# Both layers' experts by seven products of quarters, first products ahead of down

## The chip, the cores and the metric

The kernel runs on one core of one Trainium2 chip, in fp32 throughout. The metric is the device time of one execution in microseconds (us); shown is the median of several. Engines are called as in the profile: PE is TensorE, PEld its weight loads, DVE VectorE, ACT ScalarE, POOL GpSimd, SP SyncE, which here only issues transfers.

## The reference

A trunk of two layers works on 1024 tokens of width 1024 (and 256 context rows in layer 0). Each layer has a mixer (layer 0: differential and neighbourhood attention; layer 1: windowed attention and a state space scan) and then a feed-forward part by 16 experts of which each chooses its rows. That part is all that the change touches in earnest:

```python
def expert_choice_ffn(h, w_router, w_gate, w_up, w_down):
    b, n, _ = h.shape
    cap = CAPACITY_FACTOR * n // N_EXPERTS
    aff = jax.nn.softmax(jnp.einsum('bnd,de->bne', h, w_router).astype(jnp.float32), axis=-1)
    gate, idx = lax.top_k(jnp.swapaxes(aff, 1, 2), cap)
    bidx = jnp.arange(b)[:, None, None]
    xg = h[bidx, idx]
    hid = jax.nn.silu(jnp.einsum('becd,edf->becf', xg, w_gate)) * jnp.einsum('becd,edf->becf', xg, w_up)
    out = jnp.einsum('becf,efd->becd', hid, w_down) * gate[..., None].astype(h.dtype)
    return jnp.zeros_like(h).at[bidx, idx].add(out)
```

Each expert takes 128 of the 1024 tokens; in layer 0 it takes 32 of the 256 context rows too. Its three weights are 1024x1024, 4 MB each, so 12 MB are read per expert, 16 times in each layer.

## The kernel before

The program is a chain of stages, one after the other; each stage has one instruction list per engine, ordered by semaphores, and a stage's end waits for all engines. Tiles that the next stage needs early are in "Ahead" objects: they are loaded by the stage before. The experts stage of layer 0 runs from about 1010 to 1947 us, that of layer 1 from about 2676 to the end.

**Layer 0: `experts` (L2357).** An expert's rows are gathered by POOL's indirect DMA (`gather`, L2494 ff.), turned by PE against the identity (`turn_rows`), scaled and shifted from PSUM into `xT` by ACT (four blocks) and DVE (four blocks, and the context's). `xT` holds 128 token columns and 32 context columns, 160 together. Then for each of eight groups of 128 hidden features PE does eight matmuls for gate and eight for up (`hidden_rows`, L2756) with the weight as the stationary operand and the 160 columns moving. ACT takes silu of the gate half, DVE multiplies it with the up half (`hidden`, L2653): the hidden rows come out turned already, as down needs them. Down (`down_rows`, L2722) multiplies them with two halves of 512 columns, and between the halves stands the context's down (`down_ctx`, L2731), in which four stationary tiles of 32 columns are worked on side by side. ACT and DVE scale the results by the row's weight into `y` and `yc`, and POOL adds them to `moe` in HBM by a scatter with addition: first `yc`, 1 KB rows, then `y`, 4 KB rows. In POOL's loop the next expert's gather stands ahead of the scatter, and behind a wait for the last scatter.

SP loads weights by halves of columns: gate's and up's first half as soon as four feature groups are done, their second half after eight, down's two halves once the down product is over. Around the loop the stage also finishes the modulation vectors: `opening` (16 steps at its beginning, with stores by SP: `store_third`) and `closing` (8 steps at its end, whose weights SP loads into the places of gate and up). Between the first experts' loads SP runs `following.load` (L2313), which fetches what the next stage (`front`) needs, many of these transfers in 4-byte pieces, and `following.load_columns`, 4 MB of the front's weights into `following.w`.

**Layer 1: `last_experts` (L2782).** Gate and up are multiplied by seven products instead of eight: rows and weights are cut into quarters (64 rows by 512, 512 by 512), and sums of quarters are multiplied (a Strassen scheme in Winograd's form). `PRODUCTS` (L2775) is the order of the products; product 1, 2 and 3 take a quarter of the weight as it is, 5, 6, 7 and 4 take sums that DVE makes (`weight_sum`, L3017 to L3026, each over 128x2048 elements); the row sums are `row_sums`. A product (`multiply`, L3159) is 8 matmuls with 64 stationary columns and 256 moving, two side by side. Bank Z takes 5 and 3, X takes 1, 6 and 7, W takes 2, V takes 4; ACT copies a bank out in the middle of its sum (`keep`, L2953), and DVE adds that copy to a finished bank (`quarter`, L3034). `QUARTERS` says which bank and which copy make which quarter. The hidden rows come out as rows and have to be turned (`turn_hidden`, L3123) and copied by ACT into `hT` (L2976) before down (L3167), which writes into W and V once more; ACT and DVE then copy these as `y` (L2986, L3086). So the next expert's product 2 must wait for `ya` (W is copied) and product 4 for `yv` (V is copied). PE's order in the loop is: gate's seven products, up's seven, turn half the hidden rows, turn the next expert's rows, turn the other half, down with its k steps outside.

SP loads layer 1's weights by halves of rows: gate's first half after product 7, its second after product 4, and so for up; down's after the two halves of its k steps. After the last expert's gate products it loads eight blocks of `res` (`load_rows`) and then the finished sums from `moe` (`load_sum`, L2884), of which ACT takes squares (`square`, L2958) between its bank copies; at the end DVE adds them to `res` (`gated`, `summed`, L3068).

## Time and profile before

| what | us |
|---|---|
| median of 3 runs | 3416.34 (3415.37 to 3417.86) |
| the profiled execution | 3414.7 |
| its span, first to last instruction | 3413.0 |
| PE busy | 3160.0, 93% of the span |
| DVE busy | 1559.8, 46% |
| ACT busy | 1009.8, 30% |
| gate and up matmuls of layer 0 (L2756) | 301.3 and 299.4 |
| layer 0's down matmuls (L2722) | 228.3 |
| layer 1's down matmuls (L3167) | 130.8 and 129.6 |

A record of a matmul in fp32 stands twice in the counts, since each is issued as two. In the timeline, instructions of one kind are merged: `xN` is how many, the first number is the start of the first and the second the time to the end of the last, which is modelled and reaches a little into the next group; so lengths are taken from start to start. In brackets stands the idle time of the engine before it, and who ended that.

### The profile page before, as it was taken

How to read it: one execution, taken by the hardware profiler on the slowest of the kernel's cores; microseconds unless marked ns; L12 is line 12 of the kernel's file. 1: busy time of each engine (PE TensorE's matmuls, PEld its weight loads, DVE VectorE, ACT ScalarE, POOL GpSimd, SP SyncE). 2: the span in 40 equal slices, each digit the busy share in tenths (PEclk: the TensorE clock that was granted, in tenths of full speed). 3: DMA queues.
4: the chain of work that ended last, by engine and by line, in shares of the span. 5: the costliest groups of instructions: out<-in, count | busy, mean ns of one | idle time of the engine just before them, and what ended most of it. 6: DMA issues, size and time to landing. Idle time of an engine off the chain costs nothing. (4 is left out here: it accounts for less than half of the span.)

```text
span 3413.0 us, 52595 instructions
## 1 busy us (share of the span) xinstructions
PE 3160.0 (93%) x19496; PEld 2216.1 (65%) x19496; DVE 1559.8 (46%) x3170; ACT 1009.8 (30%) x2323; POOL 525.1 (15%) x639
## 2 busy tenths in 40 slices
PE   6999989999987999999999799899899299999996
PEld 4888856667435788787887565666664155555553
DVE  3212178778654010101101254566785666666565
ACT  4111156755330111101111152235554222222222
POOL 0010235110100101011110120254101101111112
PEclk9999999999987999999999899999999599999998
DMA  6336353053639977787777630100414589999996
GB/s 231 130 108 114 92 188 113 20 132 95 241 132 339 352 267 250 244 275 245 265 255 262 232 121 1 56 22 28 112 33 173 197 293 334 326 335 339 338 335 257
DMA packets 340390, 672.38 MB, mean 197 GB/s; under 512 B 84041, under 2 KB 133065, under 8 KB 334017
## 3 DMA queue, kind: packets, MB, share of 16 engines
q1 hardware_dynamic: 308384, 568.00, 47.9%
q0 software_dynamic: 13616, 47.32, 5.5%
q10 hardware_dynamic: 18240, 55.16, 4.3%
q8 instruction: 83, 1.36, 0.2%
q14 instruction: 67, 0.54, 0.1%
HBM read 585.65 MB, written 90.97 MB: 198 GB/s over the span
## 5 line engine op out<-in xcount | busy, mean ns | idle before, releaser
L2756 PE MATMUL experts_gu_ps<-experts_xT,experts_wg 128*128 128x160 f32 x2048 | 301.3, 300 | 2.6 <-DVE experts_xT L2630 2.6
L2756 PE MATMUL experts_gu_ps<-experts_xT,experts_wu 128*128 128x160 f32 x2048 | 299.4, 299 | 0.0
L2756 PEld LDWEIGHTS experts_gu_ps<-experts_xT,experts_wg 128*128 128x128 f32 x2048 | 287.9, 191 | 9.9 <-issue 9.9
L2756 PEld LDWEIGHTS experts_gu_ps<-experts_xT,experts_wu 128*128 128x128 f32 x2048 | 285.6, 190 | 0.0
L2653 DVE TENSOR_TENSOR experts_hid<-experts_sil,experts_gu_ps 128x160 f32<-128x160 f32 x128 | 41.1, 321 | 516.1 <-ACT experts_sil L2584 516.1
L2722 PE MATMUL experts_y_ps<-down_ahead_wd,experts_hid 128*128 128x512 f32 x512 | 228.3, 599 | 0.0
L2584 ACT ACTIVATE experts_sil<-experts_gu_ps 128x160 f32<-128x160 f32 x128 | 38.9, 304 | 604.9 <-PE experts_gu_ps L2756 604.9
L2722 PEld LDWEIGHTS experts_y_ps<-down_ahead_wd,experts_hid 128*128 128x128 f32 x512 | 94.6, 190 | 114.4 <-issue 113.7
L3458 PE MATMUL front_pb_ps<-kept_hT,front_ahead_w 128*128 128x512 f32 (+1 forms) x384 | 138.7, 521 | 0.7 <-DVE kept_dt L3509 0.7
L3167 PE MATMUL experts_w_ps<-experts_wd,experts_hT 128*128 128x512 f32 x256 | 130.8, 597 | 8.5 <-issue 7.8
L3167 PE MATMUL experts_v_ps<-experts_wd,experts_hT 128*128 128x512 f32 x256 | 129.6, 592 | 0.0
L2671 DVE TENSOR_SCALAR experts_y<-experts_y_ps,experts_wt 128x512 f32<-128x512 f32 x16 | 12.0, 751 | 249.0 <-PE experts_y_ps L2722 249.0
L554 PE MATMUL proj_x_ps<-first_w,first_shared 128*128 128x256 f32 x480 | 115.0, 383 | 3.1 <-DMA first_w<-in_l_w_in 3.1
L3912 PE MATMUL scan_f_ps<-scan_w,kept_hT 128*128 128x512 f32 x256 | 116.4, 597 | 0.0
L3458 PEld LDWEIGHTS front_pb_ps<-kept_hT,front_ahead_w 128*128 128x128 f32 x384 | 72.4, 190 | 62.7 <-issue 59.4
L2524 POOL DMA_INDIRECT moe<-experts_yc,experts_ixsc x16 | 25.8, 1610 | 522.5 <-ACT experts_yc L2601 522.5
L2953 ACT ACTIVATE experts_kept<-experts_x_ps 128x256 f32<-128x256 f32 x96 | 36.8, 384 | 231.7 <-PE experts_x_ps L3159 230.4
L554 PEld LDWEIGHTS proj_x_ps<-first_w,first_shared 128*128 128x128 f32 x480 | 91.7, 192 | 15.9 <-DMA first_w<-in_l_w_in 3.4
L635 DVE TENSOR_TENSOR proj_ob<-proj_z_ps,proj_kept 128x256 f32<-128x256 f32 x30 | 12.7, 424 | 190.3 <-PE proj_z_ps L554 189.5
L867 ACT ACTIVATE attn_a_e<-attn_a_e,attn_a_nmx 128x1280 f32<-128x1280 f32 (+1 forms) x80 | 96.6, 1209 | 8.0 <-DVE attn_a_e L929 8.0
L3167 PEld LDWEIGHTS experts_w_ps<-experts_wd,experts_hT 128*128 128x128 f32 x256 | 47.3, 190 | 65.5 <-issue 64.5
L3167 PEld LDWEIGHTS experts_v_ps<-experts_wd,experts_hT 128*128 128x128 f32 x256 | 48.6, 190 | 61.2 <-issue 61.2
(561 smaller groups left out, 6308.7 us busy)
## 6 DMA issues: line engine op xcount, KB each, us to landing
experts_wg<-in_l_w_gate SPq DMA_DIRECT2D x64, 2048.0 KB, 8.5
experts_wu<-in_l_w_up SPq DMA_DIRECT2D x64, 2048.0 KB, 12.7
down_ahead_wd<-in_l_w_down SPq DMA_DIRECT2D x32, 2048.0 KB, 10.6
experts_wd<-in_l_w_down SPq DMA_DIRECT2D x32, 2048.0 KB, 7.7
down_ahead_wd<-in_l_w_mod SPq DMA_DIRECT2D x16, 1024.0 KB, 9.2
proj<-proj_ob ACTq DMA_DIRECT2D x60, 256.0 KB, 2.3
first_w<-in_l_w_in SPq DMA_DIRECT2D x6, 2048.0 KB, 10.1
attn_a_mod_w<-in_l_w_mod ACTq DMA_DIRECT2D x12, 1024.0 KB, 6.5
```

The costliest lines, as they stand in the source:

```text
L554: mm = nc.tensor.matmul(to[:, left], by[k], at[k], start=(k == 0 and n in (0, 1, 5)), stop=(k == HALF - 1 and n in (3, 5, 6)), skip_group_ ...
L635: nc.vector.tensor_tensor(ob[:, slot, 0, right], Z[:, left], kept[:, 2], ALU.add).then_inc(dve_out, 1)
L867: nc.scalar.activation(e[:, s, m, 0:w], e[:, s, m, 0:w], ACT.Exp, bias=nmx[:, s, m:m + 1], scale=-1.0, accum_out=sums[:, s, m:m + 1]).then ...
L2524: pool.indirect_dma_start(moe.rearrange("t (j c) -> (t j) c", j=4), bass.IndirectOffsetOnAxis(ap=ixsc[:, 0:1], axis=0), yc[:], None, compu ...
L2584: nc.scalar.activation(sil[:, f % 2, :], GU[f % 2][:, 0, 0:N], ACT.Silu).then_inc(sil_done, 1)
L2653: nc.vector.tensor_tensor(hid[:, f, :], sil[:, f % 2, :], GU[f % 2][:, 1, 0:N], ALU.mult).then_inc(hid_done, 1)
L2722: mm = nc.tensor.matmul(Y[h][:], hid[:, k, 0:CAPX], wd[:, h, k, :], start=(k == 0), stop=(k == KD - 1))
L2756: mm = nc.tensor.matmul(GU[f % 2][:, part, 0:N], w[:, h, k, c * P:(c + 1) * P], xT[:, k, :], start=(k == 0), stop=(k == KD - 1))
L2953: nc.scalar.activation(kept[:, KEPT.index(p), :], bank[:, 0:COLS], ACT.Copy).then_inc(act_out, 1)
L3167: return nc.tensor.matmul(Y[h][:], hT[:, k, :], w[DOWN][:, k, h * BANK:(h + 1) * BANK], start=(k == 0), stop=(k == KD - 1))
L3458: mm = nc.tensor.matmul(pb[n % 4][:, 0:width], w[:, s, k, at:at + P], hT[:, k, first:first + width], start=(k == 0), stop=(k == KD - 1))
L3912: mm = nc.tensor.matmul(F[:], kept.hT[:, k, t * P:(t + 1) * P], w[:, int(kind == "q"), k, :], start=(k == 0), stop=(k == KD - 1))
```

## The change

1. `experts` is replaced by `first_experts`: layer 0's gate and up by the same seven products for the 128 tokens, and by products of their own for the context's 32 rows, which are gathered as 128 rows of 256 columns and multiplied with 32 stationary columns, four tiles side by side (`multiply_ctx`). The weights' sums lie in the place of `following.w`, so `following.load_columns` moves from the beginning of the stage to its end.
2. `PRODUCTS` is reordered to (5, 1, 2, 4, 6, 3, 7). In both layers the next expert's gate products 5 and 1 stand ahead of down, between and behind the turns of the hidden rows; the next expert's rows are turned in the middle of up.
3. Both halves of gate's weights are loaded after gate's product 7, and both of up's after up's.
4. POOL scatters before it gathers for the next expert but one; two gathers are made ahead of the loop.
5. Layer 0's last expert scatters `y` in two halves of columns.
6. In layer 1's last expert the first four sums are loaded ahead of the rows of `res`, and DVE does two of the gate multiplications among the up quarters instead of four.
7. The semaphores of the choice of rows become one; the scan's stage loads the band's queries and keys one output earlier (`NTX - 4`).

The core of the diff (in `first_experts`, lines not quoted follow `last_experts`):

```diff
-PRODUCTS = (5, 1, 2, 6, 3, 7, 4)
+PRODUCTS = (5, 1, 2, 4, 6, 3, 7)
...
+def first_experts(nc, name, K, listed, normed, mod, g_pre, w_gate, w_up, w_down, moe, following, down, last_third):
...
+                for i in (GATE, UP):
+                    for half in range(2):
+                        load(i, half, 0)
+                opening.store_third(sp, 0)
+                sp.wait_ge(opening.multiplied, START + opening.steps)
+                load_down(0)
+                following.load(sp)
+                opening.store_third(sp, 1)
+                with sp.Fori(0, E - 1) as e:
+                    for i in (GATE, UP):
+                        sp.wait_ge(mm_done, multiplied(e, i, 7))
+                        for half in range(2):
+                            load(i, half, e + 1)
+                    sp.wait_ge(y_done, right_at(e))
+                    load_down(e + 1)
+                for i in (GATE, UP):
+                    sp.wait_ge(mm_done, multiplied(E - 1, i, 7))
+                    for n in range(4):
+                        closing.load(sp, 4 * i + n)
+                following.load_columns(sp)
...
+                with pool.Fori(0, E - 1) as e:
+                    link.turn(e, 6)
+                    chosen(e)
+                    scatter(e)
+                    gather(e + 2)
+                    pool.wait_ge(s_done, e * IX + IX)
...
+                scatter_half(E - 1, 0, ya, left_out_at(E - 1))
+                scatter_ctx(E - 1)
+                scatter_half(E - 1, 1, yv, START + E + 1)
...
+                def gates_and_up(e, last=False):
+                    weight_sum(e, UP, 7)
+                    hidden_ctx(e)
+                    after(dve, ht_done, e * 3)
+                    for q in range(4):
+                        quarter(e, GATE, q)
+                    weight_sum(e, UP, 4)
+                    for q in range(4):
+                        if q == 1 and not last:
+                            weight_sum(e + 1, GATE, 5)
+                            ctx_rows(e + 1)
+                        if q >= 2:
+                            dve.wait_ge(hid_done, hidden_at(e, q - 1))
+                        quarter(e, UP, q)
+                        hidden(e, q)
+                        if q == 1 and not last:
+                            row_sums(e + 1, True)
...
+                def multiply_ctx(e, i):
...
+                    for k in range(KD):
+                        for j in range(4):
+                            mm = nc.tensor.matmul(C[j * CAPC:(j + 1) * CAPC, i, :], xcT[:, k, :], w[i][:, k, j * CW:(j + 1) * CW],
+                                                  start=(k == 0), stop=(k == KD - 1))
...
+                def from_context_to_rows(e, following_rows):
+                    multiply_ctx(e, UP)
+                    for p in PRODUCTS[2:]:
+                        multiply(e, GATE, p)
+                    turn_hidden_ctx(e)
+                    for p in PRODUCTS:
+                        multiply(e, UP, p)
+                        if p == 4 and following_rows:
+                            turn_rows(e + 1)
+                    if following_rows:
+                        pe.wait_ge(sx_done, ctx_rows_at(e + 1))
+                    turn_hidden(e, 0)
...
+                with pe.Fori(0, E - 1) as e:
+                    from_context_to_rows(e, True)
+                    multiply(e + 1, GATE, PRODUCTS[0])
+                    turn_hidden(e, 1)
+                    multiply(e + 1, GATE, PRODUCTS[1])
+                    multiply_ctx(e + 1, GATE)
+                    pe.wait_ge(xa, START + e * 2 + 4)
+                    down_all(e)
 def last_experts(...)
...
                         sp.wait_ge(mm_done, multiplied(e, i, 7))
-                        load(i, 0, e + 1)
-                        sp.wait_ge(mm_done, multiplied(e, i, 4))
-                        load(i, 1, e + 1)
+                        for half in range(2):
+                            load(i, half, e + 1)
...
-                sp.wait_ge(mm_done, multiplied(E - 1, GATE, 4))
-                following.load_rows(sp, x)
                 sp.wait_ge(s_done, (E - 1) * 16)
...
                 for t in range(M_SLOTS):
                     load_sum(t)
+                sp.wait_ge(mm_done, multiplied(E - 1, GATE, 7))
+                following.load_rows(sp, x)
...
+                gather(1)
                 with pool.Fori(0, E - 1) as e:
...
-                    gather(e + 1)
                     pool.wait_ge(ya, START + e + 1)
                     pool.wait_ge(yv, START + e + 1)
...
+                    gather(e + 2)
                     pool.wait_ge(s_done, e * 16 + 16)
...
                 with pe.Fori(0, E - 1) as e:
-                    for i in (GATE, UP):
-                        for p in PRODUCTS:
-                            multiply(e, i, p)
+                    for p in PRODUCTS[2:]:
+                        multiply(e, GATE, p)
+                    for p in PRODUCTS:
+                        multiply(e, UP, p)
+                        if p == 4:
+                            turn_rows(e + 1)
                     turn_hidden(e, 0)
-                    turn_rows(e + 1)
+                    multiply(e + 1, GATE, PRODUCTS[0])
                     turn_hidden(e, 1)
+                    multiply(e + 1, GATE, PRODUCTS[1])
                     pe.wait_ge(dve_out, quarter_at(e, UP, 3))
```

## Rows read from the trace of the kernel before

**Rows 1.** Busy time by stretch, one expert of each layer (layer 0's first).

```profile
core 0: us, PE busy (x) PEld busy (x) DVE busy (x) ACT busy (x) POOL busy (x), PEclk, DMA share, GB/s
1611.00:1664.98 53.98, 53.98 (x370) 44.22 (x369) 5.45 (x15) 6.38 (x15) 6.19 (x10) 1.00 0.76 257
2933.71:2974.42 40.71, 40.19 (x273) 23.82 (x272) 24.89 (x25) 10.32 (x24) 4.83 (x5) 1.00 0.93 335
```

**Rows 2.** Timeline of PE, an expert of layer 0: start, length, what.

```profile
1611.00 2.34 PE L2756 MATMUL experts_gu_ps<-experts_xT,experts_wg 128*128 128x160 f32 x16
...
1645.78 1.04 PE L2711 MATMUL experts_tp_ps<-ident,experts_xg 128*128 128x128 f32 x8
...
1654.41 3.66 PE L2731 MATMUL experts_yc_ps<-down_ahead_wd,experts_hid 128*32 128x256 f32 x64
1658.01 7.13 PE L2722 MATMUL experts_y_ps<-down_ahead_wd,experts_hid 128*128 128x512 f32 x16
1664.98 0.30 PE L2756 MATMUL experts_gu_ps<-experts_xT,experts_wg 128*128 128x160 f32 x1
```

**Rows 3.** Timeline of PE, the end of an expert of layer 1.

```profile
2954.48 1.90 PE L3159 MATMUL experts_x_ps<-experts_wu,experts_sx 128*64 128x256 f32 x16
2956.21 1.90 PE L3159 MATMUL experts_v_ps<-experts_tu,experts_xT 128*64 128x256 f32 x16
2958.04 0.66 PE L3123 MATMUL experts_ht_ps<-ident,experts_hid 128*128 128x128 f32 x4
...
2959.40 0.60 PE L3123 MATMUL experts_ht_ps<-ident,experts_hid 128*128 128x128 f32 x4
2960.52 1.10 PE L3167 MATMUL experts_w_ps<-experts_wd,experts_hT 128*128 128x512 f32 x2 [0.52 <-issue]
...
2974.42 1.95 PE L3159 MATMUL experts_z_ps<-experts_tg,experts_sx 128*64 128x256 f32 x16
```

**Rows 4.** Timeline of ACT and DVE in the same expert.

```profile
2956.43 0.38 ACT L2953 ACTIVATE experts_kept<-experts_x_ps 128x256 f32<-128x256 f32 x1 [2.99 <-PE experts_x_ps L3159]
...
2974.59 0.69 ACT L2986 ACTIVATE experts_y<-experts_w_ps,experts_wt 128x512 f32<-128x512 f32 x1 [11.09 <-PE experts_v_ps L3167]
...
2957.30 0.43 DVE L3040 TENSOR_TENSOR experts_hid<-experts_hid,experts_gate 128x256 f32<-128x256 f32 x1
```

**Rows 5.** Timeline, beginnings of the two experts stages.

```profile
1068.69 4.60 PE L2756 MATMUL experts_gu_ps<-experts_xT,experts_wg 128*128 128x160 f32 x16 [2.63 <-DVE experts_xT L2630]
...
1072.35 4.19 SPq L2315 DMA_DIRECT2D front_ahead_gate<-mod  x2
...
1104.07 0.58 SPq L2432 DMA_DIRECT2D experts_wg<-in_l_w_gate  x1
...
2724.26 2.91 ACT L2945 ACTIVATE experts_xT<-experts_tp_ps,experts_shift,experts_gain 128x128 f32<-128x128 f32 x8 [49.71 <-PE experts_tp_ps L3114]
```

**Rows 6.** Timeline of PE and DVE, layer 1's last expert.

```profile
3340.84 1.95 PE L3159 MATMUL experts_z_ps<-experts_tg,experts_sx 128*64 128x256 f32 x16
...
3373.23 3.68 PE L3159 MATMUL experts_x_ps<-experts_wu,experts_sx 128*64 128x256 f32 x16 [11.45 <-ACT experts_kept L2953]
...
3379.96 4.86 DVE L3068 SCALAR_TENSOR_TENSOR experts_wg<-experts_m,experts_ms,experts_wg 128x1024 f32<-128x1024 f32 x4
...
3398.83 0.74 DVE L3101 SCALAR_TENSOR_TENSOR experts_y<-experts_w_ps,experts_wt,experts_y 128x512 f32<-128x512 f32 x1
```

**Rows 7.** The tile experts_wg from 2900 to 3300 us: its loads' landing.

```profile
DMA to landing us min/median/max: 7.7/10.3/12.8
```

**Rows 8.** DMA issues from 2933.71 to 2974.42: line, count, us to landing.

```profile
moe<-experts_y,experts_ixs POOLq DMA_INDIRECT x1, 9.5
experts_xg<-normed,experts_ixg POOLq DMA_INDIRECT x1, 9.7
```

**Rows 9.** Waits of PE (2200 to 2640), of SP (1930 to 1950): total, times, longest.

```profile
PE attn_band_tr_ps L1612 <- DMA band_ahead_k<-proj: 0.8, 1, 0.8
...
SPq L2424 <- PEq L2424: 3.5, 1, 3.5
```

More of the change, by code:

```diff
@@ L212, with __init__ @@
     SLOTS = 4
-    def __init__(self, nc, st, K, rest, accs, name="mod", places=None, w_in=None):
+    def __init__(self, nc, st, K, rest, accs, name="mod", places=None, w_in=None, bias=None, rows=None):
         self.nc, self.rest, self.accs, self.gate = nc, rest, accs, K.gate
@@ L2212 @@
 class Choice:
+    SORTED, CHOSEN, WEIGHED = 1, 2, 3
     HALF = Listed.HALF
@@ L2237, in __init__ @@
         self.bank = bank[:].rearrange("p a b -> p (a b)")[:, 0:4 * self.lanes].rearrange("p (a n) -> p a n", a=4)
-        self.sorted, self.turned, self.chosen, self.weighed = (st.sem(n) for n in ("sorted", "turned", "chosen", "weighed"))
+        self.steps, self.turned = st.sem("steps"), st.sem("turned")
     def begin(self, dve, link):
@@ L2870, in _ @@
                         sp.wait_ge(mm_done, multiplied(e, i, 7))
-                        load(i, 0, e + 1)
-                        sp.wait_ge(mm_done, multiplied(e, i, 4))
-                        load(i, 1, e + 1)
+                        for half in range(2):
+                            load(i, half, e + 1)
                     for half in range(2):
@@ L2968, in gates_and_up @@
                         if p in (1, 6):
-                            for t in squares[p // 6 * 2:p // 6 * 2 + 2]:
-                                square(t)
+                            if last:
+                                square(p // 6 * 2)
+                                square(p // 6 * 2 + 1)
+                            else:
+                                act.wait_ge(mm_done, multiplied(e, UP, 4))
+                                transposed(e + 1, p // 6)
                     for c in range(2):
@@ L3014, in weight_sum @@
                     if p == 5:
-                        for half in range(2):
-                            dve.wait_ge(w_in[i][half], START + e * 16 + 16)
+                        dve.wait_ge(w_in[i][0], START + e * 16 + 16)
                         add = nc.vector.tensor_tensor(sums_of(i, 5), b12, b11, ALU.subtract)
@@ L3040, in hidden, with gates_and_up @@
                     nc.vector.tensor_tensor(hid[:, c, h, :], hid[:, c, h, :], gate[:, c, h, :], ALU.mult).then_inc(hid_done, 1)
-                def gates_and_up(e, between=None):
-                    weight_sum(e, GATE, 4)
-                    weight_sum(e, UP, 5)
-                    quarter(e, GATE, 0)
-                    quarter(e, GATE, 1)
-                    weight_sum(e, UP, 6)
-                    quarter(e, GATE, 2)
-                    quarter(e, GATE, 3)
-                    weight_sum(e, UP, 7)
+                def gates_and_up(e, last=False):
+                    for q in range(4):
+                        quarter(e, GATE, q)
                     weight_sum(e, UP, 4)
@@ L3053, in gates_and_up, with rest_of_sums @@
                     for q in range(4):
-                        if between and q in (0, 2):
-                            between(q)
-                            between(q + 1)
+                        if q == 1 and last:
+                            for t in range(2):
+                                gated(t)
+                        elif q == 1:
+                            weight_sum(e + 1, GATE, 5)
                         quarter(e, UP, q)
                         hidden(e, q)
+                        if q == 1 and not last:
+                            row_sums(e + 1, True)
+                def rest_of_sums(e):
+                    weight_sum(e, GATE, 6)
+                    weight_sum(e, GATE, 7)
+                    row_sums(e, False)
+                    weight_sum(e, GATE, 4)
+                    for p in (5, 6, 7):
+                        weight_sum(e, UP, p)
                 def gated(t):
@@ L3985, in trunk @@
                 if with_ctx:
-                    experts(nc, f"experts{n}", K, listed, normed, mods[n], layer["g_pre_ffn"], *weights, moe, following, down, rest[3])
+                    first_experts(nc, f"experts{n}", K, listed, normed, mods[n], layer["g_pre_ffn"], *weights, moe, following, down, rest[3])
                 else:
```

874 lines of the change are left out of this document (465 added, 409 removed).

## The prediction

> **What bounds the kernel now.** I read the page first: TensorE is busy for 93% of the span, so only TensorE's own work and its idle stretches can move the end. Next the table by stretch, for one expert of each layer in steady state [rows 1]. In layer 0 the period is 53.98 us and PE is busy for all of it; the DMA share is 0.76. In layer 1 the period is 40.71 us, PE is busy for 40.19 of it, and the DMA share is 0.93. So layer 0 is bound by what TensorE has to multiply; layer 1 is too, with 0.5 us of idle time per expert and transfers close behind. Third, the timeline: where the periods go on PE [rows 2, 3], and the few places where PE stands still [rows 3, 6, 9]. The granted clock in both steady stretches is 1.00, the upper level (2.4 GHz).
>
> **Layer 0, an expert.** Removed: 16 groups of 16 gate and up matmuls on 160 columns, 1611.00 to 1645.78, 34.78 us [rows 2]. Rows and context were multiplied together there. Added: 14 quarter products. Layer 1 runs just these: one takes 1.73 us from start to start (2954.48 to 2956.21), 14 of them 24.2 [rows 3]. The context rows get multiplications of their own, one for gate and one for up, in the shape of the context's down product (128*32, 64 records), which takes 3.60 (1654.41 to 1658.01) [rows 2]: 7.2. So the core goes from 34.8 to 31.4. The down halves (6.97 each, 13.9) and the context's down (3.6) stay. Transposes: 16, of which 8 were narrow, become 20 wide ones; 12 take 1.36 (2958.04 to 2959.40), so 0.113 each and 2.3 in all [rows 3]. TensorE now changes its tile shape some 10 more times in an expert. A change shows as 1.83 instead of 1.73 between starts (2956.21 to 2958.04) [rows 3], so 0.1 each, 0.9 net of what is inside the prices above. Sum: 24.2 + 10.8 + 13.9 + 2.3 + 0.9 = 52.1, against 53.98: 1.9 saved, times 16 = **-30 us**. Bounds: changes at 0.05 give 51.6 (-38), at 0.2 they give 53.1 (-14).
>
> On those changes the Trainium skill speaks against this edit (TensorEngine Tiling (Array Packing), Key Properties): changing the tiling mode, not merely the tile, drains the TensorE. It gives no figure. The trace agrees with the 0.10 above; were a drain dearer between 64 and 32 columns than the 64 to 128 that the trace has, rival D holds.
>
> The work that hides the rest: VectorE gets 8 weight sums of about 2.3 us and some 8 us of small work, 27 us in 52, and layer 1 already does as much in 40. The turned second half of the hidden rows now needs VectorE's last product 2.5 us after the seventh product ends; in layer 1 product 5 of the next expert (1.7) and the first turns (0.5 and the change) lie in between. From [rows 4], ACT keeps the bank and VectorE's multiply starts 2.8 us after that product's start; two more steps end at 4.0, and PE gets there at 4.2. So I cost that wait at nothing; if the cover is short it is 0.3 per expert.
>
> **Layer 0, first expert.** ACT alone now scales eight turned blocks, 2.91 as in layer 1 [rows 5], where it had four and VectorE the other four: half of that, +1.4. The larger term is SP's queue. Before, expert 1's weights are asked for at 1104.07 [rows 5], behind `following.load`, which starts at 1072.35: 32 us for many small transfers. They were needed only a whole period, 54 us, after the first product (1068.69). Now the gate weights may be loaded only after expert 0's gate products, and the SP must first pass `following.load` and the second `store_third`, whose four small stores have to land. I put that at 1105 to 1107. VectorE must have the first half (7.7 [rows 7]) and one sum (2.3) before product 5 of expert 1 can run: 1116 to 1118. PE has finished expert 0's up products at 1068.7 + 1.4 + 2.4 (cold start: 4.60 for a group of 2.2 [rows 5]) + 33 (products, two context groups, turns) = 1105.5. Wait: **+10.6**, bounds 3 to 18. After an idle stretch of 11.45 the first product took 3.68 instead of 1.73, as at the lower of the two clock levels [rows 6]; with the next one's share I add +2.7.
>
> **Layer 0, last expert and hand-over.** There is no next product to put between the turns: the 2.5 us and the copies are exposed, 2.9, less the turned rows of a superfluous next expert, 1.2: +1.7. The scatter in two halves makes the last transfer half as long; but SP, once the scatter had landed, still waited 3.5 us for the others at the block's end [rows 9], for the closing modulation. That chain (8 multiply steps, bias, stores) is unchanged. So the halves bring 0; at most the 0.5 that I can't see. The front's weight columns (4 MB) are now fetched at the end, after 8 MB of modulation weights from the last up product on, 12.6 MB at 360 GB/s (335 at a share of 0.93 [rows 1]) = 35 us, of which 20 lie under down and its turns, and the front turns and multiplies ten blocks of rows before it needs them: 0. Layer 0: -30 + 1.4 + 10.6 + 2.7 + 1.7 = **-13.6**.
>
> **Scan to band.** The queries are loaded one output earlier. PE waits 0.8 for the keys at the band's start [rows 9]; the queries' wait ends with the block anyway. **-0.8**.
>
> **Layer 1, the loop (15 periods).** Removed: 0.52 idle before down, since the hidden rows' copies now lie under product 1 of the next expert. Added: product 2 is now the first after down, and it writes the bank from which ACT has yet to copy y. ACT starts that 0.17 after down's end (2974.42) and takes 0.69 [rows 4], so PE waits until 0.94 after it; today products 5 and 1 cover this. Sum: 24.2 products, 8 turns with two changes 1.08, twice 4 turns 1.3, into down 0.1, down 13.9 (2960.52 to 2974.42 [rows 3]), wait 0.94, restart 0.05 = 41.55, against 40.71. +0.84 times 15 = **+12.6**; bounds 0.3 to 1.4 each (+5 to +21). First expert: product 4 comes before its sum is ready, +0.4.
>
> Weights: both halves are asked for when the seventh product ends, 9.7 after down's end. The first lands at the earliest 7.7 later [rows 7]. VectorE's sum of it (2.3) sits before the quarter that waits for up product 3, due 12 after the request, so landing must come by 9.7. The gather of rows is now issued behind the scatter (issued 1.7 after down's end, when y is copied); scatter and gather share one queue and land 9.5 and 9.7 after issue [rows 8]. I take the gather to move right behind the scatter, 10.5 to 14 after down's end, wanted at 16.5, and to delay the gate's first half by 1.2: 8.9 of the 9.7. Cost 0, with little to spare.
>
> **The tail.** Before, SP puts eight row loads (4 MB) ahead of the four sums; ACT's squares of these stand between two bank copies, so PE idles 11.45 and then runs cold [rows 6]. Now the sums go first, as soon as the last loop's scatter has landed, 1.7 + 9.5 = 11.2 after that down's end (3340.84); half a MB is there some 3.5 later, about when ACT asks (13.5), and that stall goes. What is late next: the row loads. VectorE sums from the time all eight rows are in: 6.3 MB and a MB of gathers from 11.8 after the down's end, at 360 GB/s, = 32. Before, it started at 39.1 (3379.96 less 3340.84). From there to the last piece (3398.83) it took 18.9 [rows 6], with four of eight products done ahead; now two, 1.5 us longer net of idle. So 49.6 instead of 58.0: **-8.5**, bounds -4 to -11. The last 14 us are as before.
>
> **The sum.** -13.6 - 0.8 + 0.4 + 12.6 - 8.5 = -9.9. The profiled execution took 3414.7 (span 3413.0); so 3404.8. The median of the runs is 1.6 above that execution: **3406 us**.
>
> **Rivals.**
> A, the forecast: 3406, own range 3396 to 3416.
> B, no new waits: SP is through by 1095 (its queue was slow only because weight loads were in front of it), and the wait for y is not seen, because the matmuls' own queue covers it. Gone are 13.3 and 14.1: 3379. For it: the 32 us hold 4 MB of down weights, asked for just before, which take 12 at 360 GB/s. Against it: those stand in front again, and ACT's copy of y starts 0.17 after down's end, which no reordering of PE can hasten [rows 4].
> C, slower: layer 1's weight loads become the bound. Place: VectorE's sum for product 5, between two up quarters, which holds back the hidden rows and then PE. If the gather takes its turn from the gate load and that lands at the median of 10.3 plus 1.2 [rows 7], it is 1.8 late, 15 times: +27, 3433. It decides from a landing of 9.7 on; 0.7 us beyond it, 15 times, eats the whole gain. For it: DMA share 0.93. Against: SP's queue is empty when the first half is asked for, and the shortest landing (7.7) is of that kind. Beside it, the Trainium skill (DMA: Bandwidth & Descriptors, on arbitration) says that an engine takes its queues in turn, packet by packet; by that rule the gather costs the load its own length and no more, which is what I took.
> D, shape changes cost 0.2 each: layer 0 saves 14 instead of 30: 3422. For it: the step from turns into down costs 1.12 for four turns [rows 3], 0.67 more than they take; against: 0.52 of this is a wait.
>
> **Chances.** A 0.45, B 0.20, C 0.15, D 0.20. 0.2% (6.8 us) is about what a measurement tells from no change: faster means below 3409.5, slower above 3423. A gives 0.3 faster and 0.15 same; B faster; C slower; D mostly same with 0.05 slower. Faster 0.50, same 0.30, slower 0.20. Range from near B to C: 3382 to 3432.
>
> **What would show it.** Layer 0's period at 52.1, with three context groups of 3.6 in it (53 or more: D). An idle stretch of about 10 us on PE near 1106 after the up products of expert 0, released through a weight sum or its hidden rows (none: B). In layer 1 a period of 41.5 with PE's only wait of 0.9 before product 2, released by ACT's y (40.6: B; above 42, with VectorE waiting for a load: C). The 11 us stall in the last expert gone, and VectorE's final sums starting some 32 us after the last loop's down. I am wrong if layer 0 gains nothing, or if layer 1's loop gets shorter.

## The result and the profile after

The changed kernel takes 3437.61 us (median of 4 runs, 3434.27 to 3443.01); the kernel before, run beside it, 3416.69 (4 runs, 3415.37 to 3417.86). The ratio is 1.0064, 95% interval 1.005 to 1.0077: 21 us slower. The forecast was 3406, with a range to 3432; both its sign and its range were wrong.

The profiled execution has a span of 3432.5, 19.5 more than before. Its timeline, cut at the same events as before, says where:

| stretch (us) | before | after | difference | predicted |
|---|---|---|---|---|
| start to layer 0's first product | 1068.69 | 1069.41 | +0.7 | +1.4 |
| to the closing modulation | 866.3 | 872.4 | **+6.1** | **-15.0** |
| to layer 1's first product | 792.8 | 791.5 | -1.3 | -0.8 |
| to the end of the last loop's down | 613.1 | 633.0 | **+19.9** | **+13.0** |
| to the end | 72.2 | 66.2 | -5.9 | -8.5 |

(The forecast's -13.6 for layer 0 is in the first two rows: its 1.4 for ACT's blocks falls before the first product.)

First the busy time by stretch, of one expert of each layer (the columns are those of [rows 1]):

```profile
1499.99:1553.38 53.39, 52.66 (x470) 29.60 (x468) 25.99 (x29) 11.44 (x27) 7.94 (x10) 1.00 0.73 261
2823.53:2865.34 41.81, 40.98 (x272) 23.43 (x272) 24.98 (x25) 10.30 (x25) 5.16 (x5) 1.00 0.90 326
```

Layer 0's period is 53.39 where 52.1 was expected; over 14 experts (1125.84 to 1874.03, context product to context product) the mean is 53.44, so 0.54 is saved per expert and not 1.9. And PE, which before was busy for all of the period, now stands still for 0.73 of it. Layer 1's is 41.81, with 0.84 idle. PE's waits in the execution name both places (in all, times, longest):

```profile
PE experts_ht_ps L2824 <- DVE experts_xcT L2688: 16.6, 5, 13.0
PE experts_w_ps L3332 <- ACT experts_y L3153: 12.7, 15, 0.9
PE experts_ht_ps L2824 <- issue: 7.4, 10, 0.8
```

The second was forecast. The first holds the one long stall of 13.0 in expert 0, also forecast; its other four and the ten of the third row are one and the same wait, in 14 of layer 0's experts. PE's timeline around it:

```profile
1541.10 1.09 PE L2813 MATMUL experts_tp_ps<-ident,experts_xg 128*128 128x128 f32 x8
1542.03 0.38 PE L2815 MATMUL experts_ht_ps<-ident,experts_xc 128*128 128x128 f32 x2
...
1545.85 1.90 PE L2867 MATMUL experts_x_ps<-experts_wu,experts_sx 128*64 128x256 f32 x16
1548.48 0.63 PE L2824 MATMUL experts_ht_ps<-ident,experts_gate 128*128 128x128 f32 x4 [0.73 <-issue]
1549.04 1.95 PE L2867 MATMUL experts_z_ps<-front_ahead_w,experts_sx 128*64 128x256 f32 x16
1550.92 0.66 PE L2824 MATMUL experts_ht_ps<-ident,experts_gate 128*128 128x128 f32 x4
1551.50 1.95 PE L2867 MATMUL experts_x_ps<-experts_wg,experts_xT 128*64 128x256 f32 x16
1553.38 0.85 PE L2879 MATMUL experts_c_ps<-experts_wg,experts_xcT 128*32 128x256 f32 x12
```

The rows say "issue", that is, nothing that the profile could connect. Read VectorE's timeline beside it: the first half of the hidden rows, which these transposes want, is made at the end of a chain that begins with a weight load.

```profile
1544.50 2.29 DVE L2709 TENSOR_TENSOR front_ahead_w<-experts_wg 128x2048 f32<-128x2048 f32 x1 [3.94 <-DMA experts_wg<-in_l_w_gate]
1546.71 0.42 DVE L2687 TENSOR_TENSOR experts_xcT<-experts_ht_ps,experts_gain 128x256 f32<-128x256 f32 x1
1547.16 0.42 DVE L2688 TENSOR_TENSOR experts_xcT<-experts_xcT,experts_shift 128x256 f32<-128x256 f32 x1
1547.50 0.42 DVE L2729 TENSOR_TENSOR experts_up<-experts_z_ps,experts_kept 128x256 f32<-128x256 f32 x1
1547.95 0.43 DVE L2735 TENSOR_TENSOR experts_gate<-experts_gate,experts_up 128x256 f32<-128x256 f32 x1
```

SP asks for the next gate weights when gate product 7 is done:

```profile
1521.40 1.00 SPq L2511 DMA_DIRECT2D down_ahead_wd<-in_l_w_down  x2
1533.94 0.93 SPq L2505 DMA_DIRECT2D experts_wg<-in_l_w_gate  x2
```

From 1533.94 it is 10.6 to VectorE's start at 1544.50, then 2.2 for the sum, 0.8 for the context rows, 0.9 for the up quarter and its hidden row: ready near 1548.4, and PE starts at 1548.48. Without this wait PE would have started at 1547.7. VectorE has stood idle for 3.94 before the load, while the context rows' bank was full from 1542.4 on.

Expert 0's stall came where it was forecast. The load is issued at 1106.83 (forecast 1105 to 1107); product 5 starts at 1119.89, later than the forecast's 1116 to 1118, because the turns ahead of it wait for the same chain on VectorE, context rows included:

```profile
1103.81 1.33 SPq L257 DMA_DIRECT2D mod<-experts_y  x4
1106.83 1.03 SPq L2505 DMA_DIRECT2D experts_wg<-in_l_w_gate  x2
```

```profile
1118.87 1.09 PE L2824 MATMUL experts_ht_ps<-ident,experts_gate 128*128 128x128 f32 x4 [13.02 <-DVE experts_xcT L2688]
1119.89 3.56 PE L2867 MATMUL experts_z_ps<-front_ahead_w,experts_sx 128*64 128x256 f32 x16
```

Layer 1, PE and then ACT at the end of a down product (compare [rows 3, 4]):

```profile
2845.58 0.66 PE L3296 MATMUL experts_ht_ps<-ident,experts_hid 128*128 128x128 f32 x4
2846.16 1.95 PE L3332 MATMUL experts_z_ps<-experts_tg,experts_sx 128*64 128x256 f32 x16
2848.04 0.66 PE L3296 MATMUL experts_ht_ps<-ident,experts_hid 128*128 128x128 f32 x4
...
2865.34 1.95 PE L3332 MATMUL experts_w_ps<-experts_wg,experts_xT 128*64 128x256 f32 x16 [0.84 <-ACT experts_y L3153]
```

```profile
2864.60 0.69 ACT L3153 ACTIVATE experts_y<-experts_w_ps,experts_wt 128x512 f32<-128x512 f32 x1 [13.52 <-PE experts_v_ps L3340]
```

And the tail, on PE, SP and VectorE (compare [rows 6]): no 11.45 before an up product, and VectorE now waits for the row loads.

```profile
3367.20 1.95 PE L3332 MATMUL experts_w_ps<-experts_wg,experts_xT 128*64 128x256 f32 x16 [0.93 <-ACT experts_y L3153]
```

```profile
3378.04 1.77 SPq L3038 DMA_DIRECT2D experts_m<-moe  x4
3379.85 4.36 SPq L2354 DMA_DIRECT2D experts_wg<-res  x8
```

```profile
3399.31 2.48 DVE L3244 SCALAR_TENSOR_TENSOR experts_wg<-experts_m,experts_ms,experts_wg 128x1024 f32<-128x1024 f32 x2 [8.97 <-DMA experts_wg<-res]
...
3418.34 0.75 DVE L3274 SCALAR_TENSOR_TENSOR experts_y<-experts_w_ps,experts_wt,experts_y 128x512 f32<-128x512 f32 x1
```

### The profile page after: what moved, and what is told of

Same layout as the page of the kernel before. It is cut to its first block and busy times, and to the rows that moved or that the text cites. A ratio compares the mean times of both kernels' runs of the same rounds, so it can differ in the third digit from the quotient of the medians.

```text
span 3432.5 us, 57324 instructions
## 1 busy us (share of the span) xinstructions
PE 3145.4 (92%) x21080; PEld 1977.3 (58%) x21080; DVE 1886.1 (55%) x3373; ACT 1087.3 (32%) x2510; POOL 556.4 (16%) x644
## 5 line engine op out<-in xcount | busy, mean ns | idle before, releaser
L2887 PE MATMUL experts_w_ps<-down_ahead_wd,experts_hT 128*128 128x512 f32 x256 | 114.1, 599 | 0.7 <-ACT experts_hT L2652 0.7
L2887 PE MATMUL experts_v_ps<-down_ahead_wd,experts_hT 128*128 128x512 f32 x256 | 114.1, 599 | 0.0
L2625 ACT ACTIVATE experts_kept<-experts_x_ps 128x256 f32<-128x256 f32 x96 | 36.9, 384 | 203.0 <-PE experts_x_ps L2867 203.0
L3073 POOL DMA_INDIRECT moe<-experts_y,experts_ixs x15 | 24.2, 1614 | 463.2 <-DVE experts_y L3259 463.2
L3110 ACT ACTIVATE experts_kept<-experts_x_ps 128x256 f32<-128x256 f32 x96 | 36.9, 384 | 179.9 <-PE experts_x_ps L3332 176.8
L929 DVE TENSOR_SCALAR_CACHE_REDUCE attn_a_e<-attn_a_s_ps,attn_a_nmx 128x256 f32<-128x256 f32 (+1 forms) x128 | 72.8, 613 | 29.6 <-PE attn_a_s_ps L1004 29.6
L1029 PE MATMUL attn_a_o_ps<-attn_a_v,attn_a_aT 128*128 128x128 f32 x672 | 83.6, 278 | 3.9 <-ACT attn_a_sq L882 3.9
L2617 ACT ACTIVATE experts_xT<-experts_tp_ps,experts_shift,experts_gain 128x128 f32<-128x128 f32 x128 | 48.0, 459 | 120.5 <-PE experts_ht_ps L2815 120.5
L2796 DVE TENSOR_SCALAR experts_y<-experts_v_ps,experts_wt 128x512 f32<-128x512 f32 x15 | 11.3, 752 | 135.8 <-PE experts_v_ps L2887 135.8
L1029 PEld LDWEIGHTS attn_a_o_ps<-attn_a_v,attn_a_aT 128*128 128x128 f32 x672 | 78.6, 193 | 11.4 <-issue 7.7
L3102 ACT ACTIVATE experts_xT<-experts_tp_ps,experts_shift,experts_gain 128x128 f32<-128x128 f32 x128 | 48.0, 460 | 109.9 <-PE experts_tp_ps L3287 109.9
```

Source lines behind the costliest of these rows:

```text
L929: nc.vector.tensor_scalar(e[:, s, m, c:c + w], S[i % 2][m][:, 0:w], -1.0, nmx[:, s, m:m + 1] if j else None, ALU.mult, ALU.min, accum_out= ...
L1029: mm = nc.tensor.matmul(O[:, 0:P], aT[:, kt, :], v[:, h % 2, kt, :], start=(kt * P == keys(t)[0]), stop=(kt == last))
L2617: a = nc.scalar.activation(xT[:, k, :], TP[k // 4][:, k % 4, :], ACT.Identity, bias=shift[:, 0, k:k + 1], scale=gain[:, 0, k:k + 1])
L2625: nc.scalar.activation(kept[:, KEPT.index(p), :], bank[:, 0:COLS], ACT.Copy).then_inc(act_out, 1)
L2887: mm = nc.tensor.matmul(Y[h][:], hT[:, k, :], wd[:, h, k, :], start=(k == 0), stop=(k == KD - 1))
L3102: a = nc.scalar.activation(xT[:, k, :], TP[k // 4][:, k % 4, :], ACT.Identity, bias=shift[:, k:k + 1], scale=gain[:, k:k + 1])
```

## The experiments

Each was timed beside the kernel before, whose medians in the three series were 3416.28, 3415.97 and 3417.02. Single runs of the kernel before lie within some 7 us on either side of its median, so a difference of 2 or 3 us between two medians tells nothing; for those the periods in the traces are read.

**Each layer alone.** The first of two kernels has the changed `first_experts` and the old `last_experts`, the second the other way round:

```
-    first_experts(...)   # quarters        -    last_experts(...)   # products ahead of down
+    experts(...)         # as before       +    last_experts(...)   # as before
```

> Layer 0 with its quarter products and halves of the scatter as changed, layer 1's experts as before the change. Read off the changed kernel's trace, layer 1's first product stands 5.6 us later than before; the theory (the two layers' costs add, nothing in one depends on the other) gives before + 5.6 = 3422. Rival: layer 0 only looks dear because something in the changed kernel's later stages disturbs it, or the front gives more back; then it lies within 2 us of before (3415 to 3419).

> Layer 0's experts as before the change, layer 1's as changed. Theory: from layer 1's first product to the end the changed kernel takes 13.9 us more (loop 15 x 1.11 = 16.6, the tail less), so before + 14 to 15 = 3431. Layer 1's period is 41.8. Rival: a good part of the loss comes from the hand-over of layer 0; then this is before + 8 or less (3425).

Layer 0 alone: 3421.28 us, ratio 1.0012 (1.0003 to 1.0021). Layer 1 alone: 3429.95, ratio 1.0035 (1.0021 to 1.0049). So +5.0 and +13.7, 18.7 of the 21; nothing of size lies between the layers. Layer 1's rival falls. Layer 0's (within 2 us of before) is outside the median but just inside the interval, whose lower end is +1.0; against it stands the trace of layer 0 alone, where PE has the same stall in expert 0 (13.3) and the same waits of up to 0.8 before the first turns. Each layer can be mended by itself.

**Layer 1: another bank first behind down.**

```
+    ORDER = ((5, 1, 6, 2, 4, 3, 7), PRODUCTS)     # gate, up
-    for p in PRODUCTS[2:]:
+    for p in ORDER[GATE][2:]:
         multiply(e, GATE, p)
```

> The changed kernel, but in layer 1 product 6 of the gate (bank X) comes first behind down and product 2 (bank W) second. Theory: PE's wait of 0.93 before product 2 is for ACT's copy of y out of bank W, and goes; period 41.82 to 40.9, 15 times 0.93 = -14: 3424. Rival (C of the prediction): with that wait gone the gate weights' load, for which VectorE already stands 1.7 us, is what comes late, and PE waits before the first turns instead: period 41.4 or more, at most -6: 3431.

It ran at 3422.04 us, 1.0016 (1.0007 to 1.0025), 15.6 below the changed kernel. Busy time by stretch, one expert of layer 1:

```profile
2824.60:2865.51 40.91, 40.91 (x274) 23.43 (x273) 24.98 (x25) 10.20 (x24) 4.25 (x5) 1.00 0.93 334
```

PE is busy for the whole period, 0.9 shorter, and has no wait left in the loop: the whole 0.84 to 0.93 was ACT's copy out of bank W. The load wait did not come in its place. But 40.91 is still 0.20 above the 40.71 of [rows 1], though before there were 0.52 idle: the new order costs 0.7 per expert in work of PE's own.

**Layer 0: the context rows ahead of the sum that waits for the load.**

```
                         if q == 1 and not last:
-                            weight_sum(e + 1, GATE, 5)
                             ctx_rows(e + 1)
+                            weight_sum(e + 1, GATE, 5)
```

> The changed kernel, but in layer 0 VectorE moves the next expert's context rows out of their bank before, not behind, the weight sum that waits for the gate load. Theory: PE's 0.73 of idle time before the first turns of the hidden rows is VectorE's chain load, sum, context rows, up quarter, hidden row; it is 0.9 shorter now, so the idle time goes; period 53.44 to 52.7, 15 times: -11, 3426.5. Rival: the 0.73 is TensorE's own (its queue and the change of tile shape); then the period stays at 53.4 and the time at 3437.

It ran at 3423.75 us, 1.0023 (1.0014 to 1.0032), 13.9 below the changed kernel. An expert of layer 0 by stretch, and PE and VectorE in the expert before it:

```profile
1546.09:1598.74 52.65, 52.65 (x474) 29.62 (x474) 26.19 (x29) 11.43 (x27) 7.93 (x10) 1.00 0.74 265
```

```profile
1539.33 1.90 PE L2867 MATMUL experts_x_ps<-experts_wu,experts_sx 128*64 128x256 f32 x16
1541.16 0.66 PE L2824 MATMUL experts_ht_ps<-ident,experts_gate 128*128 128x128 f32 x4
```

```profile
1537.80 2.29 DVE L2709 TENSOR_TENSOR front_ahead_w<-experts_wg 128x2048 f32<-128x2048 f32 x1 [0.98 <-DMA experts_wg<-in_l_w_gate]
1540.01 0.42 DVE L2729 TENSOR_TENSOR experts_up<-experts_z_ps,experts_kept 128x256 f32<-128x256 f32 x1
```

The "issue" was no time of TensorE's own. VectorE's load wait is still there (now 0.98 just before the sum), but the hidden row is ready in time; the mean period goes from 53.44 to 52.65, by exactly the mean wait of 0.79 (11.0 in 14 experts). That is 11 us of idle time from two instructions of 0.42 standing in the wrong place. The same order had made expert 0's stall longer: it is 11.40 here, for 13.02.

**Layer 0: two changes of tile shape fewer.**

```
                 def down_all(e):
+                    down_ctx(e)
                     down_rows(e, 0)
-                    down_ctx(e)
                     down_rows(e, 1)
```

> The changed kernel, but the context's down product comes first of the three down groups, next to the context's gate product, which has the same tile shape: two changes of shape fewer per expert (32 to 128 columns and back). Theory: a change costs 0.11 wherever it is (the period's excess over its products, turns and the idle time is 1.54 for 14 changes), so the period goes from 53.44 to 53.2: 16 x 0.22 = -3.5, 3434. Rival D of the prediction: changes to and from the narrow shape cost 0.2 and more: -7 or more, 3430. Rival: the matmuls' own queue hides a change, nothing is lost by it: 3437.5.

It ran at 3430.93 us, 1.0047 (1.0033 to 1.006). The medians say -6.7, which by itself is nearer to rival D's -7 than to the theory's -3.5; the two profiled spans say -3.3 (3432.5 to 3429.2), and the intervals of this kernel and the changed one overlap. So the price is read from PE's timeline:

```profile
1497.28 3.66 PE L2879 MATMUL experts_c_ps<-experts_wg,experts_xcT 128*32 128x256 f32 x64
1500.76 3.64 PE L2895 MATMUL experts_tp_ps<-down_ahead_wd,experts_hcT 128*32 128x256 f32 x64
1504.33 7.13 PE L2887 MATMUL experts_w_ps<-down_ahead_wd,experts_hT 128*128 128x512 f32 x16
1511.30 7.03 PE L2887 MATMUL experts_v_ps<-down_ahead_wd,experts_hT 128*128 128x512 f32 x16
1518.26 3.66 PE L2879 MATMUL experts_c_ps<-experts_wu,experts_xcT 128*32 128x256 f32 x64
```

From the first to the last of these rows it is 20.98; in the changed kernel the same four groups, alternating, take 21.31 (1499.99 to 1521.30). Both figures are the same within 0.01 in all 14 experts. That is 0.33 for two changes, 0.17 each: more than the 0.11 of the theory and less than D's 0.2; that nothing is lost by one is excluded. The period itself falls by 0.23 only, from 53.44 to 53.21, since PE's wait before the first turns grows from 0.79 to 0.89 on average: the gate load reaches VectorE later after its request, 10.9 in one expert (1530.89 to 1541.77) for 10.6. Why was not traced. The Trainium skill (TensorEngine Tiling (Array Packing), Key Properties) has TensorE drained whenever the tiling mode changes. The traces agree that each change costs time, and 0.33 for two of them is the price here.

**Layer 0's first expert: the front's column reads out of the way.**

```
 load_down(0)
+opening.store_third(sp, 1)
 following.load(sp)              # now without shift and gain
-opening.store_third(sp, 1)
 (weights of expert 1, gate and up)
+following.load_vectors(sp)      # shift, gain, g
```

> The changed kernel, but in layer 0 SP issues the front's 20 us of column reads (shift, gain) behind the loads of expert 1's gate and up weights instead of ahead of them, the rest of the front's small loads still ahead. Theory: SP's queue alone makes the 13.02 us of idle time in expert 0; the gate weights are asked for at about 1092 instead of 1106.8, the idle time falls to below 1 and the cold restart (3.56 for a product of 1.77) goes: -14, 3423.5. Rival: the stall moves, because the down weights of expert 1 now wait behind the column reads, or the gate load takes longer beside them: at most half of it, 3430.

3435.61 us, 1.0064 (1.005 to 1.0078): neither the theory's 3423.5 nor the rival's 3430. The store was moved too, and SP then stood until 1083.82 for its landing, and the plain loads took until 1103.75. The gate weights were asked for only 3.1 earlier; 10.01 of the 13.02 stayed.

**All four together.** The four edits above in one kernel.

> The changed kernel with the four mends together: other bank first in layer 1, context rows first in layer 0, the front's column reads behind expert 1's loads, context groups next to each other. Theory: each acts in a place of its own, so the gains add: -15.6 and -13.9 (both measured), -14 and -3.5 (expected): 3391, which would be 25 below before. Rival: in layer 0 they share one reserve, the time between asking for the gate weights and their landing; with a shorter period VectorE's load wait comes back and a third of it is lost: 3400.

3405.36 us, 0.9972 (0.9961 to 0.9982), 32 below the changed kernel and 11 below the one before. The parts were worth 15.6, 13.9, 2.0 and, by the spans, 3.3, together 35: they add, nearly. What is missing against 3391 is the stall that the column reads did not cause; PE still waited 9.55 in expert 0.

**Layer 0's first expert: all of the front's loads behind weight loads.**

```
 load_down(0)
-following.load(sp)
 opening.store_third(sp, 1)
+load_next(0, following.load)             # behind expert 1's gate and up
+load_next(1, following.load_vectors)     # behind expert 2's
```

> The changed kernel, but in layer 0 all of the front's small loads are issued behind weight loads: the plain ones behind expert 1's gate and up weights, the column reads behind expert 2's; ahead of expert 1's gate weights stands only the store of the second third. The run that moved the column reads alone kept 10.0 of the 13.0 us: SP then waited 8.5 for the stores to land, and needed 20 us for the plain loads, up to 1103.75. Theory: those 20 us are the rest of the stall; the gate weights are asked for at about 1092 and the idle time falls to below 1, the cold restart goes: 13.6 below the changed kernel, 3424. Rival: what holds the gate weights is not SP's queue but the 4 MB of down weights and the stores in front of them, in the transfers themselves; then the idle time stays at 5 or more: 3430.

3424.84 us (median of nine executions), 1.0024 (1.0015 to 1.0034), 12.8 below the changed kernel; a tenth execution took 14083.65, and nothing on record says why. SP and PE:

```profile
1091.87 0.94 SPq L2507 DMA_DIRECT2D experts_wg<-in_l_w_gate  x2
```

```profile
1103.88 1.90 PE L2876 MATMUL experts_x_ps<-experts_wu,experts_sx 128*64 128x256 f32 x16
1105.71 0.66 PE L2833 MATMUL experts_ht_ps<-ident,experts_gate 128*128 128x128 f32 x4
...
1162.48 0.63 PE L2833 MATMUL experts_ht_ps<-ident,experts_gate 128*128 128x128 f32 x4 [4.09 <-DVE experts_xcT L2697]
```

SP's queue was the stall: with the weights asked for at 1091.87 it is gone, although the 4 MB of down weights and the stores are in front of them as ever. But a piece came back one expert later, 4.09 where 0.8 is usual. The small loads ran until 1134.5, so the down weights were asked for only at 1134.54. The gate weights behind them were asked for in time, at 1144.43, but reached VectorE 14.1 later, at 1158.50, where 10.6 is usual.

**The scatter in one piece.**

```
-scatter_half(E - 1, 0, ya, left_out_at(E - 1))
-scatter_ctx(E - 1)
-scatter_half(E - 1, 1, yv, START + E + 1)
+scatter(E - 1)
```

> The changed kernel, but layer 0's last expert scatters whole rows in one transfer, behind the context's. Theory: the block's end is set by the closing modulation, not by the scatter; the halves bring nothing: 3437.6, within 2 us. Rival: the first half, under way 10 us earlier, was hidden work that the block's end now waits for: +3, 3441.

3433.86 us, 1.0053 (1.004 to 1.0067), an interval that overlaps the changed kernel's. From the closing modulation's first product to the front's first transposes the two traces have 25.24 (one piece) and 25.15 (halves); the difference in span (2.5) stands before the scatter, where the code is the same (1.6 of it before layer 0's first product). The halves bring nothing that these runs can show.

**The tail alone.** The kernel before, with the four sums asked for ahead of the rows:

```
-sp.wait_ge(mm_done, multiplied(E - 1, GATE, 4))
-following.load_rows(sp, x)
 sp.wait_ge(s_done, (E - 1) * 16)
 ...
 for t in range(M_SLOTS):
     load_sum(t)
+sp.wait_ge(mm_done, multiplied(E - 1, GATE, 4))
+following.load_rows(sp, x)
```

> The kernel before, with one thing of the change: SP asks for the four sums ahead of the eight row loads in the last expert. Theory: the stall of 11.45 goes, the row loads become what is late, all in 32 to 33 us after the last loop's down instead of 39.1: -6, 3410. Rival: PE's stall hid nothing that counts and the end is set by the eight sums and their squares on ACT and VectorE: within 1 us of before.

3409.42 us, 0.9982 (0.9973 to 0.9991): 6.6 faster. On PE the longest wait of the last expert is 1.28; VectorE's final sums begin at 3372.76, when the rows have landed, 32.9 after the down's end (3339.91), then need 18.8:

```profile
3372.76 4.87 DVE L3068 SCALAR_TENSOR_TENSOR experts_wg<-experts_m,experts_ms,experts_wg 128x1024 f32<-128x1024 f32 x4 [6.65 <-DMA experts_wg<-res]
```

**Everything that helped, in one kernel.** The mends of layer 1 and layer 0 with the front's loads spread, and a second kernel that moves `gated(2)` and `gated(3)` ahead of VectorE's wait for the rows.

> All mends together: other bank first in layer 1, context rows first and context groups adjacent in layer 0, and all of the front's small loads behind the weight loads of experts 1 and 2. The four together ran at 3405.4 with 9.6 us of idle time and a cold restart left in expert 0. Theory: these go, -11: 3394. Rival: the front's loads now delay expert 2's or 3's weights, the stall comes back there: 3402.

> As final, and in the tail VectorE multiplies rows 2 and 3 by the gate before, not behind, its wait for the row loads, in which it stands idle for 9 us. Theory: two products of 1.22 leave the stretch between the landing of the rows and the end: -2.4 against final, 3391.6. Rival: the squares of the later sums and GpSimd's steps on them set the pace from the third row on (VectorE waits 0.5 for GpSimd in each of the last rows), and most of it is given back: -1, 3393.

The first: 3399.02 us, 0.9946 (0.9932 to 0.996), 38.6 below the changed kernel and 18 below the one before. Of the 11 that the last mend was to add, 6.3 came; the stall's echo in expert 1 is 2.7 here. The second: 3397.46, 0.9934 (0.9919 to 0.9949), not to be told from the first; in its trace the stretch from the rows' landing to the last piece is 19.15 against 18.82. VectorE now stands 1.91 there for a square of ACT's and 2.58 in four waits for GpSimd, where the first kernel has 1.80 in three waits for GpSimd alone. So the two products moved ahead were given back, and the rival holds.

## Why the prediction was wrong

**Layer 0's period, the step that failed.** "52.1, against 53.98: 1.9 saved, times 16 = -30": it is 53.44, so 8.6. Two terms made up the 1.34: a wait that was put at nothing, and a price that was too small.

- 0.79 is a wait that I costed at nothing. The text said "the work that hides the rest": VectorE has 27 us of work in 52, and layer 1 does as much in 40. That counts busy time, and the wait was one of order. I traced the turned second half (product 5, ACT's copy, the hidden row) and did work out the weight load's landing, but in layer 1 alone, "8.9 of the 9.7", where the measurement gave 8.3 (2832.58 to 2840.91) and no wait of PE's (VectorE stood 2.23 for it). In layer 0 the same load takes 10.6, and two context operations stand behind it that layer 1 does not have. Rival C was the right mechanism at the wrong layer. The exchanged order on VectorE, and nothing else, took the 0.79 away.
- The other 0.55 is changes of tile shape. I read their price from [rows 3] as 1.83 against 1.73, 0.10. That is only what shows ahead of a change. The product behind one takes 1.78, another 0.05, and between two groups of turns it is 1.88 from start to start (1549.04 to 1550.92 above). With some 10 changes more than before, 0.05 each is 0.5; removing two gave 0.33, so 0.17 each where I had 0.10. D, with 0.20, had the direction and somewhat too large a step.

**The rest of layer 0 held, in part by luck.** From the first product on there are 14.8 of losses outside the period, against 15.0 predicted (10.6 + 2.7 + 1.7). The parts are less close. The stall was 13.02 for 10.6, with the queue where I had put it: VectorE had the load after 8.1 (1106.83 to 1114.89) for my 7.7, but behind its sum came the context rows and the up quarter, 1.7, the same order that costs the 0.79. The slow restart was 2.1 for 2.7: product 5 took 3.49 from start to start for 1.88, the turns 1.02 for 0.56, at a granted clock of 0.52 from 1118.87 to 1123.38. The stall's cause is shown: it went when the gate weights were issued at 1091.87. B falls with it. Of ACT's 1.4 ahead of the first product little shows: from the first turn to that product it is 5.89, for 5.56 before.

**Layer 1's loop: right mechanism, size off, one item forgotten.** The wait before product 2 was 0.84 to 0.93 for 0.94, by ACT's copy as said, and went with the bank. The period is 41.81 for 41.55. Most of the 0.26 is the same short price: the period has eight changes, and each costs some 0.05 more than I gave it. And I multiplied 0.84 by 15 but left out that the last loop's down now comes behind two products of expert 15 (3.46), which the tail, costed by its transfers, does not give back. 1.10 times 15 is 16.5, and with the 3.5 it is 20.0, where 19.9 was measured.

**The tail.** Rows in 33.0 after the down's end for my 32; from there 19.0, for 18.9 before. The step's own terms (32 + 18.9 + 1.5 = 52.4 against 58.0) make -5.6; the -8.5 in the text was a slip of addition. Measured: -5.9. The 1.5 for the two gate products that now come last did not show, since VectorE's other waits in that stretch fell from 4.2 to 2.0. No share of the change's other parts shows: alone in the old kernel the move gave 6.6.

**The halves of the scatter, and scan to band.** The halves gave 0, as said. The -1.3 for -0.8 bears nothing out: the stretch from the closing modulation to layer 1's first product is 792.8 and 791.3 in the two kernels without the earlier loads (the one before and the tail alone), and 790.8 to 796.4 in the twelve with them. At the place itself the loads did harm, PE's wait for the queries' rows before and after:

```profile
2405.38 1.97 PE L1612 MATMUL attn_band_tr_ps<-ident,band_ahead_q 128*128 128x128 f32 x8 [9.56 <-DMA band_ahead_q<-proj]
```

```profile
2412.40 1.94 PE L1612 MATMUL attn_band_tr_ps<-ident,band_ahead_q 128*128 128x128 f32 x8 [13.17 <-PEq L3836]
```

The first row is the kernel before, the second the changed one. From the start of the scan's last products (2393.92 and 2397.34) to these it is 11.46 and 15.06. It is 11.40 in the tail alone, and 14.62 to 15.63 in all twelve with the earlier loads. The keys' wait of 0.75 did go, but PE's wait for the queries, 9.56, became one of 13.17 for the end of the scan's block (L3836), and I had put that block's end down as unchanged. What makes it later is open, and taking this part back was not tried.

Against the sum of -9.9: layer 0 +21.1, layer 1's loop +6.9, the tail +2.6, the start -0.7 and scan to band -0.5 add up to +29.4, which makes +19.5. The causes stood in C (0.15) and D (0.2), but each with one place and one price, and none of the cases had both at once.

## What to carry to other kernels

An engine that is half idle can still be what holds the bound engine: follow its instructions in their order from the last thing that lands (here a load) to what the bound engine wants, and move whatever does not need that load ahead of it. Behind a long product put first the one whose bank no other engine has yet to empty. When small products replace large ones, write down the sequence of tile shapes and price every change in it on both its sides; and when work is pulled ahead of a loop's body, count what the last turn then does more.

## What was not expected of the hardware

- A change of tile shape between 64 and 128 columns costs PE some 0.15 us, in two parts: the product ahead of it takes 0.10 longer from start to start, the one behind it 0.05 (1.73, 1.83 and 1.78 for a quarter product). Changes between 32 and 128 columns cost about as much, 0.17 (21.31 less 20.98, for two).
- Issuing one small transfer can hold SP for long, here always with transfers of MBs asked for before it: one of the front's column reads kept it 10.85 us (in the run with the column reads out of the way), one of the projection weights 10.09 (in the run with all loads spread), where most take 0.6. Whether and which transfers in front cause it was not measured.
- The same load of 2 MB halves needed 10.6 us to VectorE's start in layer 0 and 8.3 in layer 1, at DMA shares of 0.73 and 0.90. The lower share had the longer landing; in layer 0 4 MB of down weights were asked for 12.5 before it. Whether these were its cause stays open.
